# Layer crossings with their rows, gated outputs and scaled chunks in PSUM banks, part of the squares added by TensorE, and three slots first

## The chip, the cores and the metric

One core of a Trainium2 chip runs the whole program. The time is the device time of one execution in microseconds. The engines are TensorE (PE in the profile), VectorE (DVE), ScalarE (ACT), GpSimd (POOL) and SyncE (SP).

## The reference, cut to what matters

The program computes one hybrid block on 512 tokens and then four layers on 512 latent and 256 context tokens, 1024 features wide: windowed attention (layer 0), MLA (1), mLSTM (2), windowed attention (3). What the change touches is what stands between two of the four layers:

```python
for i in range(4):
    h_l = rmsnorm(x_lat, g_pre) * (1.0 + sc_l) + sh_l
    h_c = rmsnorm(x_ctx, g_pre) * (1.0 + sc_c) + sh_c
    y_l, y_c = mixer(h_l, h_c, ...)          # begins with h @ w_in, ends with (...) @ w_out
    x_lat = x_lat + gt_l * rmsnorm(y_l, g_post)
    if need_ctx:
        x_ctx = x_ctx + gt_c * rmsnorm(y_c, g_post)
```

A crossing, as it is called here, is from `@ w_out` of one layer to `@ w_in` of the next, in latent tokens (512 columns, LAT) and in context tokens (256 columns, CTX). There are three. In each, for each of the two parts: the squares of y are summed over 1024 features and give one rstd a token; y is gated and added to x; the squares of the new x are summed and give the next rstd; x is scaled, shifted and split into a high and a low part for the products.

## The kernel before

Activations lie feature-major: 8 chunks (KC) of 128 features, tokens along the columns. fp32 products are made of three fast products of high and low parts (`products`, L459 to L461). Weights come in slots of 1 MB in one fixed stream. Three ring places hold slots (a fourth slot of each output projection has its own place). For each slot SyncE issues the load once the slot before it in its place is used up, ScalarE makes the high part (`refill_hi`, L454; the tile after which it does so is in `refills`), and GpSimd the low part (`low_part`, L446), in the order of the stream.

`dense` (L486) runs one or more sections. TensorE makes the tiles in order, each in the next of `n_banks` PSUM banks, and waits for the bank's last user. ScalarE takes each tile out (`act_tile`); with `dve_tile` VectorE works on it next and frees the bank. If `n_banks` differs from the section before, TensorE first waits until all banks are free. With `lead` n the first n tiles are made together, chunk by chunk, each chunk when `rhs_ready` says that its low part is there. A `side` object puts work between the tiles: `half_tensor` in the middle of a tile, `on_tensor` after one, `on_scalar` after ScalarE's taking, `on_vector` ahead of VectorE's part, `after_scalar` and `after_vector` at the end. Everything on one engine runs in the order in which it is written.

`layer_cross` (L2744) runs the output projection on 7 banks: 8 latent tiles, then 8 context tiles. VectorE squares each latent tile and adds it to `total` (L2787, L2788); for the context ScalarE squares from PSUM (L2779) and VectorE adds (L2785). `LatentCrossing` stands as a side in the context tiles 8 to 15:

- TensorE sums `total` over the partitions with ones (`sum_up`, L2572) after tile 8, into bank 7. ScalarE makes rstd (`root`: Ln, L971, and Exp, L974), VectorE gates y in place and adds it to x (`residual`, L2587 and L2592), two chunks a tile.
- ScalarE squares the new x into `wide` (L2598), VectorE gathers the squares in `total` (L2604, L2607), TensorE sums them in the middle of tile 15, ScalarE makes the second rstd after tile 14.
- VectorE scales into `wide` (L2614), ScalarE shifts and makes the high part (L2619), VectorE the low part (L2624), chunk by chunk, with four buffers in `wide`.

`ContextCrossing` does the same for 256 columns inside the next section: the MLA's input section `Bin` (2 slots), the mLSTM's value section `Cv` (4 slots, 24 tiles with 256 columns), layer 3's query section `A3q` (4 slots, 8 latent tiles). Its places are given by `hosted`. In `Bin` and `Cv` two slots are used for the latent tiles first, then the same two for the context tiles. `LatentSteps` is the MLA's own side work; it stands in `Bz`.

## Time and profile before

| | |
|---|---|
| median of 3 runs | 2998.2 us (2993.7 to 3003.2) |
| the profiled execution, its span | 3006.05 us, 3004.4 us |
| TensorE busy | 2799.1 us, 93% |
| VectorE busy | 1571.7 us, 52% |
| ScalarE busy | 1231.1 us, 41% |
| GpSimd busy | 880.1 us, 29% |
| TensorE's mean granted clock | 0.976 of full |

Shares are of the span. A timeline row has the start in us, the time in us, engine, line, operation, output <- inputs, sizes and, in brackets, how long the engine stood before it and who ended that. "x2" is two instructions in a row, with one time for both. Weight loads of TensorE have rows of their own, named PEld. The three crossings begin at 1668, 2090 and 2598 us.

### The profile page before, as it was taken

How to read it: one execution, taken by the hardware profiler on the slowest of the kernel's cores; microseconds unless marked ns; L12 is line 12 of the kernel's file. 1: busy time of each engine (PE TensorE's matmuls, PEld its weight loads, DVE VectorE, ACT ScalarE, POOL GpSimd, SP SyncE). 2: the span in 40 equal slices, each digit the busy share in tenths (PEclk: the TensorE clock that was granted, in tenths of full speed). 3: DMA queues.
4: the chain of work that ended last, by engine and by line, in shares of the span. 5: the costliest groups of instructions: out<-in, count | busy, mean ns of one | idle time of the engine just before them, and what ended most of it. 6: DMA issues, size and time to landing. Idle time of an engine off the chain costs nothing.

```text
span 3004.4 us, 40540 instructions
## 1 busy us (share of the span) xinstructions
PE 2799.1 (93%) x16296; PEld 2329.7 (78%) x16296; DVE 1571.7 (52%) x3138; ACT 1231.1 (41%) x2139; POOL 880.1 (29%) x636
## 2 busy tenths in 40 slices
PE   6989989999999999999999979999899999989997
PEld 4766878778877788878877768677798998878785
DVE  6677290162942776660278461354627238562583
ACT  4335224453213222242278354544443326343582
POOL 3611564404543444423300123200223320124301
PEclk8999999999999999999999989999999999999998
DMA  7303452301323555531200221101112331123101
GB/s 312 138 28 120 182 210 84 112 1 70 128 101 129 215 190 191 204 147 71 92 15 2 78 81 67 43 1 57 71 58 71 142 126 55 71 85 127 49 2 70
DMA packets 55450, 300.09 MB, mean 100 GB/s; under 512 B 4640, under 2 KB 9056, under 8 KB 25440
## 3 DMA queue, kind: packets, MB, share of 16 engines
q1 hardware_dynamic: 22464, 163.59, 15.2%
q10 hardware_dynamic: 32800, 133.92, 11.8%
q8 instruction: 129, 2.11, 0.3%
q14 instruction: 57, 0.47, 0.0%
HBM read 271.25 MB, written 21.00 MB: 97 GB/s over the span
## 4 chain that ended last, share of the span: by engine, by line
PE 57%; DVE 11%; ACT 3%; issue 2%; DMA 0%; PEldq 0%; DVEq 0%; PEld 0%; ACTq 0%
PE psum L459 14%; PE psum L460 14%; PE psum L461 14%; PE psum L1889 2%; PE psum L3510 2%; PE psum L1729 2%; PE psum L1752 2%; PE psum L1910 2%; DVE pair_row L1943 1%; PE psum L1899 1%; DVE y L2587 1%; PE psum L1733 1%; PE psum L1741 1%; DVE total L2607 1%; DVE pair_prob L1952 1%
## 5 line engine op out<-in xcount | busy, mean ns | idle before, releaser
L446 POOL TENSOR_TENSOR w_lo<-raw,w_hi 128x512 fp32r<-128x512 f32 x612 | 853.6, 1426 | 2065.7 <-ACT w_hi L454 2065.7
L459 PE MATMUL psum<-a_hi,w_hi 128*128 128x512 f32 (+1 forms) x1848 | 697.6, 377 | 50.3 <-DVE a_lo L1132 18.4
L460 PE MATMUL psum<-a_lo,w_hi 128*128 128x512 f32 (+1 forms) x1848 | 686.6, 372 | 0.0
L461 PE MATMUL psum<-a_hi,w_lo 128*128 128x512 f32 (+1 forms) x1848 | 686.2, 371 | 0.0
L459 PEld LDWEIGHTS psum<-a_hi,w_hi 128*128 128x128 f32 x1848 | 350.7, 190 | 122.5 <-issue 24.1
L460 PEld LDWEIGHTS psum<-a_lo,w_hi 128*128 128x128 f32 x1848 | 350.8, 190 | 63.2 <-issue 3.4
L461 PEld LDWEIGHTS psum<-a_hi,w_lo 128*128 128x128 f32 x1848 | 350.4, 190 | 61.7
L454 ACT ACTIVATE w_hi<-raw 128x2048 fp32r<-128x2048 f32 x153 | 292.5, 1912 | 250.1 <-DMA raw<-stream 217.3
L459 PE MATMUL psum<-w_hi,a_hi 128*128 128x256 f32 x800 | 232.8, 291 | 4.9 <-DVE a_lo L2624 4.2
L460 PE MATMUL psum<-w_lo,a_hi 128*128 128x256 f32 x800 | 228.1, 285 | 0.0
L461 PE MATMUL psum<-w_hi,a_lo 128*128 128x256 f32 x800 | 228.0, 285 | 0.0
L875 DVE SCALAR_TENSOR_TENSOR ada_temp<-ada_ring,psum 128x1024 f32<-128x1024 f32 x160 | 185.7, 1215 | 29.3 <-ACT psum L1104 15.2
L459 PEld LDWEIGHTS psum<-w_hi,a_hi 128*128 128x128 f32 x800 | 155.1, 194 | 8.5 <-issue 5.1
L460 PEld LDWEIGHTS psum<-w_lo,a_hi 128*128 128x128 f32 x800 | 155.4, 194 | 1.6 <-issue 1.4
L461 PEld LDWEIGHTS psum<-w_hi,a_lo 128*128 128x128 f32 x800 | 155.3, 194 | 0.0
L875 DVE SCALAR_TENSOR_TENSOR ada_temp<-ada_ring,ada_rows 128x1024 f32<-128x1024 f32 x80 | 129.4, 1674 | 35.7 <-DVEq L1481 16.0
L1943 DVE CUSTOM_DVE_ANT_0 pair_row<-psum,pair_mask,neg_sinks 128x512 f32<-128x512 f32 (+2 forms) x160 | 116.6, 747 | 41.0 <-PE psum L1889 28.0
L1971 ACT ACTIVATE pair_prob<-pair_row,pair_stat 128x513 f32<-128x513 f32 (+2 forms) x160 | 114.8, 719 | 45.7 <-PE psum L1899 25.8
L1889 PE MATMUL psum<-gk,gq 64*128 64x128 f32 (+1 forms) x960 | 94.8, 330 | 13.3 <-DVE pair_stat L1943 11.5
L459 PE MATMUL psum<-hid_hi,w_hi 128*128 128x512 f32 x256 | 99.8, 390 | 0.0
L460 PE MATMUL psum<-hid_lo,w_hi 128*128 128x512 f32 x256 | 99.6, 389 | 0.0
L461 PE MATMUL psum<-hid_hi,w_lo 128*128 128x512 f32 x256 | 99.6, 389 | 0.0
(430 smaller groups left out, 4736.9 us busy)
## 6 DMA issues: line engine op xcount, KB each, us to landing
raw<-stream SPq DMA_DIRECT2D x153, 1024.0 KB, 4.8
ada_ring<-ada ACTq DMA_DIRECT2D x72, 1024.0 KB, 5.8
x_in<-xres ACTq DMA_DIRECT2D x3, 3072.0 KB, 12.5
xres<-x_in ACTq DMA_DIRECT2D x3, 2048.0 KB, 6.8
gates<-gate_part ACTq DMA_DIRECT2D x8, 768.0 KB, 3.9
partner<-gq ACTq DMA_DIRECT2D x4, 1024.0 KB, 9.2
xres<-x_in ACTq DMA_DIRECT2D x1, 3072.0 KB, 9.4
own_raw<-stream SPq DMA_DIRECT2D x3, 1024.0 KB, 5.0
```

The lines of the kernel that those rows point to most:

```text
L446: last = pool.tensor_tensor(k.lo_of(s)[:, cols], k.raw_of(s)[:, cols], k.hi_of(s)[:, cols].bitcast(F32), ALU.subtract)
L454: act.activation(k.hi_of(s), k.raw_of(s), ACT.Copy).then_inc(k.hi_ready, 1)
L459: pe.matmul(out, lhs[0], rhs[0], start=start, stop=False)
L460: pe.matmul(out, lhs[0], rhs[1], start=False, stop=False)
L461: return pe.matmul(out, lhs[1], rhs[0], start=False, stop=stop)
L875: dve.scalar_tensor_tensor(self.temp[:, self.products % 2], self.ring[:, place, c], 1.0, self.used_rows[:, w], ALU.mult, ALU.mult, accum_o ...
L1729: pe.matmul(score(u)[:, col:col + cols], q, keys, start=True, stop=False)
L1752: last = pe.matmul(value_bank(u), units[u]["pv"][j], prob_t[:, u % n_t, j * P:(j + 1) * P], start=j == 0, stop=j == n_blocks - 1)
L1889: last = pe.matmul(score(u)[:, col:col + cols], q, keys, start=True, stop=True)
L1910: last = pe.matmul(k.psum[64 * (u % 2):64 * (u % 2) + 64, 7, 0:P], units[u]["pv"][j], prob_t[:, u % 4, j * P:(j + 1) * P], start=j == 0, s ...
L1943: dve.tensor_tensor_reduce(row[:, u % 4, 1:1 + w], score(u), mask[:, un["mask"]:un["mask"] + w], 1.0, un["sink"], ALU.add, ALU.min, stat[: ...
L1971: act.activation(prob[:, u % 4, 0:1 + width(u)], row[:, u % 4, 0:1 + width(u)], ACT.Exp, bias=stat[:, 0, u % 4:u % 4 + 1], scale=-1.0, acc ...
```

## The change

In words, and then the diff cut to its core:

- Tiles keep banks 0 to 3 (`n_banks=4`) in the output projection and in the sections that follow it (`Bin` and `Bz`, `Cv`, the sections of layer 3). Bank 4 holds sums and then rstd of the latent part, bank 5 those of the context; banks 6 and 7 (`held`) hold gated outputs, two chunks in turn, and then scaled chunks.
- TensorE adds the last latent square to `total`, all 8 context squares of y straight from `square_c`, three of the 8 squares of the new latent x, and all 8 of the new context x. VectorE gathers five latent squares only (`GATHERED`).
- The latent sum stands in the middle of tile 8 and of tile 14; ScalarE's roots stand ahead of its taking of tiles 8 and 15 (`early_scalar`). VectorE's crossing work stands in one piece after its last latent square.
- The next section's third slot is made ready at the end of the crossing, and three slots are used for the latent tiles and then for the context tiles in `Bin` with the first of `Bz` (the two are one section now), and in `Cv`.

```diff
@@ dense
+                        if side is not None and 2 * (j + 1) == len(slot_tiles[0][1]):
+                            side.half_tensor(pe, 0)
...
+                    if side is not None:
+                        side.early_scalar(act, t)
                     if act_tile is not None:
                         act.wait_ge(done.sem, done_at(t))
-                        act_tile(act, i, tt, bank(t)).then_inc((free if dve_tile is None else staged).sem, 1)
+                        act_tile(act, i, tt, bank(t)) \
+                            .then_inc((free if dve_tile is None or t >= dve_until else staged).sem, 1)
...
-                if dve_tile is not None:
+                if dve_tile is not None and t < dve_until:
@@ class Crossing
+        self.sums = self.rstd = k.psum[:, 4 + n, 0:self.w]
...
+    def held(self, c):
+
+        return self.k.psum[:, 6 + c % 2, 0:self.w]
...
     def root(self, act, turn):
+
+        act.preload_act_table_set("natural_log")
         act.wait_ge(self.summed.sem, self.summed.at(turn + 1))
-        root_rows(self.k, act, self.rstd, [(self.t0, self.t1)], D, (7,))
-        act.nop().then_inc(self.rooted.sem, 1)
+        self.k.act_chain(act, act.activation(self.logs, self.sums, ACT.Ln, bias=self.k.eps[:], scale=1.0 / D))
+        act.activation(self.rstd, self.logs, ACT.Exp, scale=-0.5).then_inc(self.rooted.sem, 1)
...
         for j in (c, c + 1):
-            y = self.part(self.y, j)
-            gated = k.dve_chain.mark(dve.scalar_tensor_tensor(y, y, k.gate2[:, self.l, j, self.n:self.n + 1],
-                                                              self.rstd[:, self.t0:self.t1], ALU.mult, ALU.mult))
+            if j >= 2:
+                dve.wait_ge(self.added.sem, self.added.at(j - 1))
+            gated = k.dve_chain.mark(dve.scalar_tensor_tensor(self.held(j), self.part(self.y, j),
+                                                              k.gate2[:, self.l, j, self.n:self.n + 1], self.rstd,
+                                                              ALU.mult, ALU.mult))
...
+    def scale(self, dve, c):
+        if c == 0:
+            dve.wait_ge(self.rooted.sem, self.rooted.at(2))
+        if c >= 2:
+            dve.wait_ge(self.low.sem, self.low.at(c - 1))
+        dve.scalar_tensor_tensor(self.held(c), self.part(self.x, c), self.coef(c), self.rstd,
+                                 ALU.mult, ALU.mult).then_inc(self.scaled.sem, 1)
@@ class LatentCrossing
+    def half_tensor(self, pe, t):
+        k, q = self.k, t - KC
+        if q == 0:
+            pe.wait_ge(k.tile_free.sem, self.tile_free + KC)
+            pe.matmul(self.sums, k.cst("ones"), self.total, start=True, stop=False)
+            pe.matmul(self.sums, k.cst("ones"), self.last_square, start=False, stop=True).then_inc(self.summed.sem, 1)
+        if q >= 1:
+            self.context.sum_square(pe, q - 1)
+        if q == 6:
+            pe.wait_ge(self.gathered.sem, self.gathered.at(GATHERED))
+            pe.wait_ge(self.squared.sem, self.squared.at(KC - 1))
+            pe.matmul(self.sums, k.cst("ones"), self.total, start=True, stop=False)
+            for c in range(GATHERED + 1, KC):
+                if c == KC - 1:
+                    pe.wait_ge(self.squared.sem, self.squared.at(KC))
+                last = pe.matmul(self.sums, k.cst("ones"), self.wide[:, c % 4], start=False, stop=c == KC - 1)
+            last.then_inc(self.summed.sem, 1)
+
+    def early_scalar(self, act, t):
+        if t == KC:
+            self.root(act, 0)
+        if t == KC + 7:
+            self.root(act, 1)
...
     def after_vector(self, dve):
+        self.residual(dve, 0)
+        self.residual(dve, 2)
+        self.gather(dve, 1)
+        self.residual(dve, 4)
+        self.gather(dve, 2)
+        self.gather(dve, 3)
+        self.residual(dve, 6)
+        self.gather(dve, 4)
+        self.norm(dve)
@@ class ContextCrossing
+    def sum_square(self, pe, c):
+        k = self.k
+        pe.wait_ge(k.tile_free.sem, self.tile_free + KC + c + 1)
+        last = pe.matmul(self.sums, k.cst("ones"), self.own_squares[:, c % 4], start=c == 0, stop=c == KC - 1)
+        last.then_inc((self.partial if c < KC - 1 else self.summed).sem, 1)
+
+    def half_tensor(self, pe, t):
+        if t == 0:
+            self.sum_square(pe, KC - 1)
...
         if t == self.sum_at:
-            self.sum_up(pe, 0)
...
+            pe.wait_ge(self.squared.sem, self.squared.at(KC))
+            for c in range(KC):
+                last = pe.matmul(self.sums, k.cst("ones"), self.wide[:, c], start=c == 0, stop=c == KC - 1)
+            last.then_inc(self.summed.sem, 1)
+
+    def early_scalar(self, act, t):
+        if t == 0:
             self.root(act, 0)
-        if t == self.square_at:
             for c in range(KC):
-                self.square(act, c)
+                act.wait_ge(self.added.sem, self.added.at(c + 1))
+                act.activation(self.wide[:, c], self.part(self.x, c), ACT.Square).then_inc(self.squared.sem, 1)
             self.store_part(act)
-        if t == self.again_at - 1:
+        if t == self.root_at:
             self.root(act, 1)
-            for c in range(KC):
+        if t in self.high_at:
+            for c in range(*self.high_at[t]):
                 self.take_high(act, c)
@@ layer_cross
-          visits=[(s, feature_major(b, KC, [part])) for part in (LAT, CTX) for s in range(4)], own=3,
-          refills={0: [first + 2], 2: [first + 3], KC + 3: [first + 4], KC + 5: [first + 5]})
+    dense(k, block, [section], None, act_tile=take, dve_tile=add_square, side=latent, barrier=False, n_banks=4,
+          visits=[(s, feature_major(b, KC, [part])) for part in (LAT, CTX) for s in range(4)], own=3, dve_until=KC,
+          refills={0: [first + 2], 2: [first + 3], KC + 3: [first + 4], KC + 6: [first + 5]})
@@ gqa_layer (layer 3)
-        crossing[1].hosted(0, 1, 4)
+        crossing[1].hosted(3, 4, {5: (0, 4), 6: (4, 8)})
...
-          n_banks=BANKS if both else 7, side=crossing and crossing[1])
+          n_banks=BANKS if both else 4, side=crossing and crossing[1],
+          refills=None if both else {2 * s - 2: [SECTIONS[f"A{l}q"][0] + s + 1] for s in range(2, 5)})
@@ mla_layer
+    context.hosted(3, 4, {5: (0, 4), 6: (4, 8)})
...
+    dense(k, block, ["Bin", "Bz"], None, act_tile=take_in, barrier=False, lead=2, n_banks=4,
+          side=BothSides(context, steps, 11),
+          visits=[(s, feature_major(a, KC, [part])) for part in both for s in range(3)]
+          + [(s, feature_major(a, KC, both)) for s in range(3, 6)],
+          refills={9: [first + 3], 12: [first + 4], 14: [first + 5], 17: [first + 6], 21: [first + 7]})
@@ mlstm_layer
-    dense(k, block, ["Cv"], None, barrier=False, lead=2, n_banks=7, side=context, act_tile=take_value,
+    context.hosted(7, 9, {10: (0, 4), 11: (4, 8)})
...
+    dense(k, block, ["Cv"], None, barrier=False, lead=4, n_banks=4, side=context, act_tile=take_value,
+          visits=[(s, token_major(a, bs, 256, 256)) for bs in (range(4), (4, 5)) for s in range(3)]
+          + [(3, token_major(a, range(6), 256, 256))],
+          refills={15: [first + 3], 18: [first + 4], 20: [first + 5]})
```

## Rows read from the trace of the kernel before

**Rows 1.** Who waited for whom, TensorE, whole span: us, times, longest.

```profile
PE psum L2572 <- DVE total L2607: 39.0, 6, 8.7
```

**Rows 2.** Timeline of TensorE: first product of each of the three crossings.

```profile
1668.39 0.47 PE L459 MATMUL psum<-a_hi,w_hi 128*128 128x512 f32 x1 [0.47 <-PEq L386]
...
2089.89 0.47 PE L459 MATMUL psum<-b_hi,w_hi 128*128 128x512 f32 x1 [0.46 <-PEq L386]
...
2597.89 0.47 PE L459 MATMUL psum<-b_hi,w_hi 128*128 128x512 f32 x1 [0.74 <-DVEq L391]
```

**Rows 3.** Timeline of ScalarE: a tile taken out; last ones of the sections after.

```profile
1706.80 0.60 ACT L2772 ACTIVATE y<-psum 128x512 f32<-128x512 f32 x1 [4.84 <-PE psum L461]
...
1800.36 0.38 ACT L3034 ACTIVATE m_raw<-psum 128x256 f32<-128x256 f32 x1 [2.49 <-PE psum L461]
...
2252.07 0.39 ACT L3356 ACTIVATE cv<-psum 128x256 f32<-128x256 f32 x1 [2.50 <-PE psum L461]
...
2731.22 0.60 ACT L2828 ACTIVATE gq<-psum 128x512 f32<-128x512 f32 x1 [1.81 <-PE psum L461]
```

**Rows 4.** Timeline of TensorE in crossing 1: its long waits.

```profile
1743.35 2.08 PE L2572 MATMUL psum<-total,const 128*128 128x512 f32 x2 [8.71 <-DVE total L2607]
...
1750.79 0.47 PE L459 MATMUL psum<-a_hi,w_hi 128*128 128x512 f32 x1 [2.81 <-DVE a_lo L2624]
...
1780.53 1.22 PE L2572 MATMUL psum<-total,const 128*128 128x256 f32 x2 [8.34 <-DVE total L2607]
```

**Rows 5.** Stretch: us, busy PE, PEld, DVE, ACT, POOL, granted clock, DMA share, GB/s.

```profile
1735.00:1751.00 16.00, 4.85 (x15) 3.55 (x16) 12.74 (x13) 9.51 (x14) 9.13 (x6) 0.68 0.35 131
```

**Rows 6.** Timeline of TensorE: a ones-product, and the second product behind it.

```profile
1714.91 1.02 PE L2572 MATMUL psum<-total,const 128*128 128x512 f32 x2
...
1715.89 0.28 PE L460 MATMUL psum<-a_lo,w_hi 128*128 128x256 f32 x1
```

**Rows 7.** Timeline of VectorE: residual adds without and beside GpSimd.

```profile
1721.12 1.28 DVE L2592 TENSOR_TENSOR x_in<-x_in,y 128x512 f32<-128x512 f32 x2
...
1731.71 3.49 DVE L2592 TENSOR_TENSOR x_in<-x_in,y 128x512 f32<-128x512 f32 x2
```

**Rows 8.** By line: duration in ns min/median/max, first and last start in us.

```profile
L2334 DVE TENSOR_TENSOR psum<-psum,r x32: 690/698/700, 978.5 to 1274.6; 128x512 f32<-128x512 f32 x32
...
L2787 DVE TENSOR_TENSOR square<-y x24: 682/692/1393, 1680.9 to 2642.3; 128x512 f32<-128x512 f32 x24
...
L875 DVE SCALAR_TENSOR_TENSOR ada_temp<-ada_ring,psum x160: 1206/1215/1223, 16.1 to 1306.7; 128x1024 f32<-128x1024 f32 x160
```

**Rows 9.** Timeline of ScalarE: the first latent root of crossing 1.

```profile
1715.78 1.28 ACT L971 ACT_TABLE_LOAD   x1
1717.08 0.69 ACT L971 ACTIVATE rstd_y<-psum,eps 128x512 f32<-128x512 f32 x1
1717.78 1.28 ACT L974 ACT_TABLE_LOAD   x1
```

**Rows 10.** A slot's high part, low part and load (last number: us to landing).

```profile
L454 ACT ACTIVATE w_hi<-raw 128x2048 fp32r<-128x2048 f32 x153 | 292.5, 1912 | 250.1 <-DMA raw<-stream 217.3
...
1676.69 5.04 POOL L446 TENSOR_TENSOR w_lo<-raw,w_hi 128x512 fp32r<-128x512 f32 x4 [173.78 <-ACT w_hi L454]
...
raw<-stream SPq DMA_DIRECT2D x153, 1024.0 KB, 4.8
```

**Rows 11.** Timeline: VectorE begins to scale; one of ScalarE's high parts.

```profile
1748.17 0.75 DVE L2614 SCALAR_TENSOR_TENSOR wide<-x_in,coef,rstd_y 128x512 f32<-128x512 f32 x1 [2.94 <-ACTq L2578]
...
1751.34 0.72 ACT L2619 ACTIVATE a_hi<-wide,mod 128x512 fp32r<-128x512 f32 x1 [0.60 <-DVE wide L2614]
```

**Rows 12.** Timeline of VectorE: gated context outputs of two groups in a row.

```profile
1767.22 0.88 DVE L2587 SCALAR_TENSOR_TENSOR y<-y,gate,rstd_y 128x256 f32<-128x256 f32 x2 [7.75 <-ACTq L2578]
...
1768.69 0.88 DVE L2587 SCALAR_TENSOR_TENSOR y<-y,gate,rstd_y 128x256 f32<-128x256 f32 x2
```

**Rows 13.** Chain of waits: start us, us, what; between gate and residual add.

```profile
1721.27 0.45 issue
```

More of the change, by code:

```diff
@@ L509, in dense @@
     total = n_t * turns
+    dve_until = total if dve_until is None else dve_until
     share = ada.share(total) if ada else None
@@ L2591, in residual @@
             x = self.part(self.x, j)
[L2592 to L2607 removed]
+            dve.tensor_tensor(x, x, self.held(j), ALU.add).then_inc(self.added.sem, 1)
     def scale(self, dve, c):
@@ L2618, in take_high @@
         act.wait_ge(self.scaled.sem, self.scaled.at(c + 1))
-        act.activation(self.part(self.a[0], c), self.spare(c), ACT.Identity, bias=self.shift(c)) \
+        act.activation(self.part(self.a[0], c), self.held(c), ACT.Identity, bias=self.shift(c)) \
             .then_inc(self.high.sem, 1)
@@ L2623, in take_low, with norm @@
         dve.wait_ge(self.high.sem, self.high.at(c + 1))
-        dve.scalar_tensor_tensor(self.part(self.a[1], c), self.spare(c), self.shift(c),
+        dve.scalar_tensor_tensor(self.part(self.a[1], c), self.held(c), self.shift(c),
                                  self.part(self.a[0], c).bitcast(F32), ALU.add, ALU.subtract) \
             .then_inc(self.low.sem, 1)
+    def norm(self, dve):
+        self.scale(dve, 0)
+        for c in range(KC):
+            if c + 1 < KC:
+                self.scale(dve, c + 1)
+            self.take_low(dve, c)
     def store_part(self, act):
@@ L2646, in at, with over, square @@
         return self.base + n
+GATHERED = 4
 class LatentCrossing(Crossing):
-    def on_tensor(self, pe, t):
-        if t == KC:
-            self.sum_up(pe, 0)
-    def half_tensor(self, pe, t):
-        if t == 2 * KC - 1:
-            self.sum_up(pe, 1)
+    def over(self, context, total, last_square, own_squares, tile_free, late):
+        self.context, self.total, self.last_square, self.own_squares = context, total, last_square, own_squares
+        self.tile_free, self.late = tile_free, late
+    def half_tensor(self, pe, t):
[16 more added lines that the diff above has]
+    def early_scalar(self, act, t):
+        if t == KC:
+            self.root(act, 0)
+        if t == KC + 7:
+            self.root(act, 1)
+    def square(self, act, c):
+        act.wait_ge(self.added.sem, self.added.at(c + 1))
+        if c >= 4:
+            act.wait_ge(self.gathered.sem, self.gathered.at(max(1, c - 4)))
+        act.activation(self.wide[:, c % 4], self.part(self.x, c), ACT.Square).then_inc(self.squared.sem, 1)
     def on_scalar(self, act, t):
         q = t - KC
-        if q == 0:
-            self.root(act, 0)
         if 1 <= q <= 4:
@@ L2695, with gather @@
-class ContextCrossing(Crossing):
-    def hosted(self, sum_at, square_at, again_at):
-        self.sum_at, self.square_at, self.again_at = sum_at, square_at, again_at
+        refill_hi(self.k, act, self.late)
+    def gather(self, dve, c):
+        dve.wait_ge(self.squared.sem, self.squared.at(c + 1))
+        if c == 1:
+            dve.tensor_tensor(self.total, self.wide[:, 0], self.wide[:, 1], ALU.add).then_inc(self.gathered.sem, 1)
+            return
+        dve.wait_ge(self.gathered.sem, self.gathered.at(c - 1))
+        dve.tensor_tensor(self.total, self.total, self.wide[:, c % 4], ALU.add).then_inc(self.gathered.sem, 1)
@@ L2726, in on_vector @@
     def on_vector(self, dve, t):
-        if t:
-            return
-        for c in range(0, KC, 2):
-            self.residual(dve, c)
-            if c:
-                self.gather(dve, max(1, c - 2))
-                if c > 2:
-                    self.gather(dve, c - 1)
-        self.gather(dve, KC - 2)
-        self.gather(dve, KC - 1)
-        for c in range(KC + 1):
-            if c < KC:
-                self.scale(dve, c)
-            if c:
-                self.take_low(dve, c - 1)
+        if t == 0:
+            dve.wait_ge(self.latent.low.sem, self.latent.low.at(KC))
+            for c in range(0, KC, 2):
+                self.residual(dve, c)
+            self.norm(dve)
 def layer_cross(k, block, l, section, b, a, y_at, x_at, temp):
     y, x = k.at("y", y_at, [P, KC, T2]), k.at("x_in", x_at, [P, KC, T2])
-    total = k.at("total", temp, [P, T2])
-    rstd = k.at("rstd_y", temp + 3072, [P, T2])
+    total = k.at("total", temp, [P, S])
+    logs = k.at("rstd_y", temp + 3072, [P, T2])
     square = k.at("square", temp + 6144, [P, 2, S])
@@ L2768, in layer_cross @@
     start = k.tile_free.base
+    first = SECTIONS[section][0]
+    latent = LatentCrossing(k, l, 0, y, x, a, logs[:, 0:S], wide)
+    context = ContextCrossing(k, l, 1, y, x, a, logs[:, S:T2], wide_c)
+    context.over(square_c, start, latent)
+    latent.over(context, total[:], square[:, (KC - 1) % 2], square_c, start, first + 6)
     def take(act, i, t, ps):
@@ L2974, in over, with __init__, half_tensor, on_tensor @@
             x.stage_over(n)
+class BothSides(Side):
+    def __init__(self, context, steps, at):
+        self.context, self.steps, self.at = context, steps, at
+    def half_tensor(self, pe, t):
+        self.context.half_tensor(pe, t)
+    def on_tensor(self, pe, t):
+        self.context.on_tensor(pe, t)
+        if t >= self.at:
+            self.steps.on_tensor(pe, t - self.at)
+    def early_scalar(self, act, t):
+        self.context.early_scalar(act, t)
+        if t == self.at:
+            self.context.after_scalar(act)
+    def on_scalar(self, act, t):
+        if t >= self.at:
+            self.steps.on_scalar(act, t - self.at)
+    def on_vector(self, dve, t):
+        self.context.on_vector(dve, t)
+        if t >= self.at:
+            self.steps.on_vector(dve, t - self.at)
 class QueryTurns(Side):
```

117 lines of the change are left out of this document (37 added, 80 removed).

## The prediction

> **What bounds the kernel now.** I read the list of who waited for whom on TensorE first. Over the whole span one wait stands on top of those the change can touch: the two-stage sum that closes each layer crossing waits for VectorE's adds, 39.0 us in 6 waits [rows 1]. There are three crossings. From the timeline I took where each begins (first product of the output projection) and where the section that receives the context half ends [rows 2, 3]. A 512-column tile takes 4.84 + 0.60 = 5.44 us from one eviction to the next, a 256-column tile 2.89 us [rows 3]; both are TensorE's pace. Against that pace:
>
> - Crossing 1, projection and the first MLA section: 12 tiles of each size = 99.9 us; it took 1800.8 - 1668.4 = 132.4. Excess 32.5 us.
> - Crossing 2, projection and the value section of 24 small tiles: 43.5 + 92.5 = 136.0; it took 2252.1 - 2089.9 = 162.2. Excess 26.2.
> - Crossing 3, projection and the query section of 8 large tiles: 110.2; it took 2731.2 - 2597.9 = 133.3. Excess 23.1.
>
> So 82 us in all are above TensorE's own pace. In crossing 1 TensorE waited 8.7 us for the latent sum, 2.8 for the first low part and 8.3 for the context sum [rows 4], and between 1735 and 1751 us its granted clock was 0.68 of full, so part of the stretch at 1.2 GHz and not 2.4, after the 8.7 us wait [rows 5]. That is the room. Why the sum is late shows on VectorE: two residual adds took 1.28 us while GpSimd was idle and 3.49 while it worked [rows 7].
>
> **What the change adds to TensorE.** A ones-product of 512 columns holds TensorE from 1714.91 to 1715.89, less the 0.12 of the product between (2.89 / 24): 0.86 us; 256 columns half, 0.43 [rows 6]. Per crossing before: two of each, 2.6 us. After: latent rows 2, context rows 8 small, latent new rows 4 (total and three squares), context new rows 8 small: 6 x 0.86 + 16 x 0.43 = 12.0 us, say 12.4 with the breaks. The added 9.8 us are in TensorE's stream and only pay where it stood idle anyway.
>
> **What it does to the latent chain.** An operand in PSUM costs VectorE nothing at this size: 698 ns in PSUM against 692 between SBUF tiles, and 160 operations with a PSUM operand spread from 1206 to 1223 ns only, so GpSimd doesn't disturb them [rows 8]. The context squares leave VectorE. I go through crossing 1 in its own times.
>
> 1. TensorE stops in the middle of context tile 0 (1713.5) for the last square, adds 1.75 us and gives the sum at 1715.5. ScalarE roots before it takes that tile: Ln 0.69, table load 1.28 [rows 9], Exp by estimate like Ln, 0.65: VectorE starts at 1718.3, 1.5 us earlier than now. Tile 1's break waits for the late taking, with the first wait 0.9 us.
> 2. VectorE: four pairs of residual at 2.65 us (four operations of 0.66), four adds of squares of 0.7: done at 1732 to 1733; ScalarE's last square at 1733.4.
> 3. TensorE reaches the middle of tile 6 at 1735.7 with 1.75 + 6 x 0.43 us of ones inside. Nothing waits. Four ones-products: 1739.7; the tile ends at 1741.2.
> 4. ScalarE may root only when it has taken tile 6 and made a high part: 0.66 + 1.91 [rows 10], then load, Ln, load, Exp, 3.9 us: 1747.7. Now VectorE starts scaling at 1748.17 [rows 11]. All that was won on VectorE is handed over at this place. The first low part comes at 1750.2 instead of 1750.8.
> 5. TensorE ends tile 7 at 1744.3 and stands 5.9 us. So per crossing: one wait of 5.9 for 8.7 + 2.8, and 9.8 more work.
> 6. The next section's first tiles follow the low parts. ScalarE's high parts come every 0.72 + 0.60 = 1.32 us [rows 11]; a bank that must be read before it is written again adds about 0.1. TensorE needs 1.36 per chunk, so little is lost, but after 5.9 us idle I expect the low clock for some 3.4 us of it: 1.7 us. Bounds: 0 and 3.
>
> By the end of the first tiles crossing 1 is where it was before (within 0.5 us).
>
> **Context half, crossings 1 and 3.** Root from 1761.7 to 1765.2 (after the high parts and a slot's high part of 1.91; two loads 2.56 and by estimate 0.9 for Ln and Exp at half the width of rows 9), then four groups of VectorE, 1.47 us each now [rows 12] and 1.6 with the bank waits: squares end at 1772.3. TensorE has tiles 2 and 3 until 1774.1. The wait of 8.3 us is gone. In crossing 1 the high parts 4 to 7 are made only after tile 5 is taken; the context tile that reads them loses 1.7 us (bounds 0, 3). Then the slot that follows three resident ones: free after tile 7, landed 4.8 us later, high part after tile 9 (5.8 + 0.4), 1.91, low part 5.04 [rows 10], 13.3 us against four tiles of 2.89 = 11.5: TensorE stands 1.8 us (bounds 0, 4). Another 0.8 for the clock.
> Crossing 1: 12.4 + 0.9 + 5.9 + 2.0 + 1.7 + 1.8 + 0.8 = 25.5 against 32.5: **-7.0**.
> Crossing 3 has neither of the last three (its context tiles come a section later): 12.4 + 0.9 + 5.9 + 1.9 = 21.1 against 23.1: **-2.0**.
>
> **Crossing 2.** Here the first four tiles run together and there are four banks. ScalarE makes the context root and all eight squares before it takes tile 0; TensorE needs tile 0's bank for tile 4. Behind that wait stands everything on TensorE, the context sum too. First tiles end at 2185.3 (four times 2.89, one break, the clock). ScalarE: high parts end 2180.8, slot 1.91, two loads 2.56, Ln and Exp at half the width of rows 9 by estimate 0.9: 2186.3; VectorE 6.4; last square and taking 2193.6. A new wait of 8.3 us, and 2.0 for the clock after it. Bounds: 6 (no bank waits) and 12. High parts 0.5, late slot 1.8, waiting for all banks when the next section changes from 4 to 7 banks 0.7.
> 12.4 + 0.9 + 5.9 + 1.7 + 8.3 + 2.0 + 0.5 + 1.8 + 0.7 = 34.2 against 26.2: **+8.0**.
>
> **Sum.** -7.0 - 2.0 + 8.0 = -1.0 us. Against the profiled execution's 3006.1 (span 3004.4) that is 3005.1. The runs' median is 2998.2, 7.9 under the profiled one, so I predict 2997.
>
> **Two rules of the Trainium skill.** The first: the trace shows two table loads of 1.28 us in a root, one ahead of Ln and one ahead of Exp [rows 9]. The Trainium skill, ScalarE: Activation LUTs, section "Table sets: the hidden batching unit", says that one set holds both ln and exp, so that one load serves both. The change asks for a set ahead of Ln; were it one with both, a load would go at each root (a rival below). The second: VectorE: DVE Perf Modes, section "The TRN2 errata", again the Trainium skill, charges a VectorE operation from PSUM 120 cycles instead of 58 from SBUF, by estimate 0.065 us more; on some 17 operations of the latent chain that would be 1 us more per crossing. The rows say 698 against 692 ns, and by them nothing is added.
>
> **Rivals.**
> - *Clock and waits at their kind ends (faster).* After a shorter idle of 5.9 us the clock doesn't fall, and the bank waits cost nothing: 3 x 1.8 + 2.0 + 0.8 of clock and about 2 of crossing 2's wait: -10.2, in all -11: 2987. For it: each idle is shorter than 8.7 us. Against it: the clock is low in rows 5 over a wait of 2.8 us too.
> - *Two banks make a ping-pong (slower).* From gate to add the chain shows 0.45 us in which the engine waited for nothing seen [rows 13]. If each handing over of a bank costs that and not 0.05, the latent norm is 8 x 0.4 = 3.2 us longer and TensorE follows it: 9.6 over three crossings, and 3 in crossing 2's new wait: +12.6, in all +11.6: 3010. It decides from some 0.3 us per chunk on. Against it: VectorE's own rows run without a gap across its chained waits.
> - *It doesn't do what it says.* GpSimd slows the operations with PSUM operands as it does the others: about 1 us in the residual beyond the 2.2 us to spare at step 3, and 2 in the norm beside the second slot's low part: +3 per crossing, 3006. Rows 8 speak against it.
> - *One table load per root.* The one ahead of Exp goes: 1.28 us on the second latent root of three crossings and on the context root of crossing 2: -5.1, in all -6: 2992. The rule is the Trainium skill's, named above; the trace has two loads each time.
>
> **How the numbers follow.** Forecast 0.50, kind ends 0.22, ping-pong 0.15, GpSimd 0.06, one load 0.07. A change of under 0.3% (9 us) can't be told from none here. Faster: the 0.22 and 0.05 from the forecast's own spread: 0.27. Slower: 0.15, 0.03 of the GpSimd case, 0.03 of the forecast's: 0.20 with rounding. The same: 0.53. Low and high end reach to the two outer cases: 2985 to 3011; the forecast's own range is 2990 to 3004.
>
> **What would show it.** Right: the waits of the latent and context sums for VectorE gone; one wait of 5 to 7 us ahead of each following section, released by a low part; TensorE idle 6 to 12 us at the value section's fifth tile with ScalarE's taking as releaser; 1 to 3 us for a low part from GpSimd at the fourth slot of the MLA and value sections; residual adds of 1.3 us per pair also beside GpSimd. Wrong: the second latent root before 1745 in crossing 1's times (then about 3 us per crossing more are won), no wait at the fifth tile (8 to 10 us more), or a high part every 1.7 us or more.

## The result, and the profile after

The changed kernel takes 3006.38 us (median of 16 runs, 3003.6 to 3010.0) against 2999.80 us of the kernel before (16 runs, 2992.7 to 3003.9): a ratio of 1.0023, 95% interval 1.0016 to 1.0030. It is slower by 6.6 us. The forecast was 2997 us, no measurable change. A later repetition of the unchanged pair on another chip (below) gives 1.0026.

The profiled execution of the kernel after has a span of 3003.1 us and an own time of 3005.17. TensorE is busy 2818.9 us (before 2799.1), VectorE 1520.2 (1571.7), ScalarE 1227.9, GpSimd 870.7; the mean granted clock is 0.981 (0.976).

The waits of TensorE in the kernel after, whole span (us, times, longest):

```profile
PE psum L459 <- DVE a_lo L2616: 17.4, 6, 5.6
...
PE psum L459 <- POOL w_lo L446: 13.5, 6, 4.8
...
PE psum L3590 <- DVE c_decay L3697: 10.4, 9, 1.6
...
PE psum L459 <- ACT cv L3436: 6.9, 2, 6.4
...
PE psum L2984 <- ACTq L2974: 2.6, 1, 2.6
```

The 39.0 us for sums [rows 1] are gone. The places of the others, in the timeline of TensorE; these rows answer to [rows 4]:

```profile
1747.25 0.77 PE L459 MATMUL psum<-a_hi,w_hi 128*128 128x512 f32 x1 [5.56 <-DVE a_lo L2616]
...
1807.58 0.50 PE L459 MATMUL psum<-a_hi,w_hi 128*128 128x512 f32 x1 [1.61 <-POOL w_lo L446]
...
1829.78 1.53 PE L2984 MATMUL psum<-squares,const 128*128 128x512 f32 x4 [2.63 <-ACTq L2974]
...
2164.49 0.55 PE L459 MATMUL psum<-w_hi,a_hi 128*128 128x256 f32 x1 [5.55 <-DVE a_lo L2616]
...
2185.35 0.56 PE L459 MATMUL psum<-w_hi,a_hi 128*128 128x256 f32 x1 [6.41 <-ACT cv L3436]
...
2680.43 0.77 PE L459 MATMUL psum<-a_hi,w_hi 128*128 128x512 f32 x1 [5.56 <-DVE a_lo L2616]
```

Each crossing ends in one wait of 5.6 us, released by a low part, and the value section has the new wait at its fifth tile. What stands ahead of the first of them is the timeline of ScalarE and, last, VectorE in crossing 1:

```profile
1738.43 0.38 ACT L2814 ACTIVATE y<-psum 128x256 f32<-128x256 f32 x1 [6.07 <-PE psum L461]
1738.71 0.38 ACT L2821 ACTIVATE square_c<-psum 128x256 f32<-128x256 f32 x1
1738.98 1.91 ACT L454 ACTIVATE w_hi<-raw 128x2048 fp32r<-128x2048 f32 x1
1740.91 1.28 ACT L2580 ACT_TABLE_LOAD   x1
1742.21 0.69 ACT L2582 ACTIVATE rstd_y<-psum,eps 128x512 f32<-128x512 f32 x1
1742.91 1.28 ACT L2583 ACT_TABLE_LOAD   x1
...
1744.84 1.41 DVE L2606 SCALAR_TENSOR_TENSOR psum<-x_in,coef,psum 128x512 f32<-128x512 f32 x2 [16.36 <-ACT psum L2583]
```

VectorE stood 16.36 us; its gathering had ended at 1728.5. All of its lead is lost at ScalarE, whose order is: take tile 6, convert a slot, root.

GpSimd, in turn, begins its low parts only when VectorE's latent adds are over, 0.19 us after the last of them. It is so in all three crossings of both profiles of after. The end of VectorE's gathering and GpSimd's start in crossing 1:

```profile
1727.80 0.69 DVE L2709 TENSOR_TENSOR total<-total,wide 128x512 f32<-128x512 f32 x1
...
1728.68 5.02 POOL L446 TENSOR_TENSOR w_lo<-raw,w_hi 128x512 fp32r<-128x512 f32 x4 [38.21 <-ACT w_hi L454]
```

Cut at the same events as [rows 2] and [rows 3] (first product of each projection; last tile of mz, cv, gq taken out), every profile taken in this study falls into seven stretches. "Crossing" is a projection with the section behind it. All in us:

| | start to 1 | crossing 1 | 1 to 2 | crossing 2 | 2 to 3 | crossing 3 | tail | three crossings |
|---|---|---|---|---|---|---|---|---|
| before | 1668.4 | 204.5 | 217.0 | 162.2 | 345.8 | 133.3 | 273.2 | 500.0 |
| before_again | 1667.6 | 201.4 | 219.0 | 158.9 | 345.9 | 132.0 | 272.9 | 492.2 |
| before_third | 1666.1 | 205.3 | 216.9 | 162.1 | 345.8 | 130.2 | 273.3 | 497.6 |
| before_fourth | 1665.4 | 205.3 | 216.9 | 162.1 | 345.8 | 130.3 | 273.3 | 497.6 |
| after | 1665.9 | 199.6 | 217.6 | 168.2 | 347.7 | 131.3 | 272.7 | 499.2 |
| after_again | 1663.5 | 199.6 | 221.2 | 168.2 | 347.8 | 131.3 | 272.7 | 499.0 |

The profile that the prediction was made from has the dearest crossings of four profiles of the same kernel; the changed kernel's repeat to 0.1 us. Their mean before is 496.9, after 499.1.

### The profile page after: what moved, and what is told of

Its sections match the earlier page's. It is cut to its first block, busy times and chain, and to the rows that moved or that the text cites. A ratio compares the mean times of both kernels' runs of the same rounds, so it can differ in the third digit from the quotient of the medians.

```text
span 3003.1 us, 40627 instructions
## 1 busy us (share of the span) xinstructions
PE 2818.9 (94%) x16404; PEld 2344.5 (78%) x16404; DVE 1520.2 (51%) x3081; ACT 1227.9 (41%) x2139; POOL 870.7 (29%) x636
## 4 chain that ended last, share of the span: by engine, by line
PE 59%; DVE 8%; ACT 3%; issue 1%; DMA 1%; POOL 0%; PEldq 0%; DVEq 0%; PEld 0%; ACTq 0%
PE psum L459 15%; PE psum L460 15%; PE psum L461 15%; PE psum L1898 2%; PE psum L1738 2%; PE psum L3590 2%; PE psum L1761 2%; PE psum L1919 2%; DVE pair_row L1952 1%; PE psum L1908 1%; PE psum L1742 1%; PE psum L1750 1%; DVE pair_prob L1961 1%; ACT w_hi L454 0%; DVE c_decay L3697 0%
## 5 line engine op out<-in xcount | busy, mean ns | idle before, releaser
L446 POOL TENSOR_TENSOR w_lo<-raw,w_hi 128x512 fp32r<-128x512 f32 x612 | 844.1, 1411 | 2074.0 <-ACT w_hi L454 2074.0
```

The costliest lines, as they stand in the source:

```text
L446: last = pool.tensor_tensor(k.lo_of(s)[:, cols], k.raw_of(s)[:, cols], k.hi_of(s)[:, cols].bitcast(F32), ALU.subtract)
```

## The experiments

The repetitions of before and before_splits_late start from the kernel before, every other experiment from the kernel after. Ratios are to runs of before on the same chip, with 95% intervals.

**before_again and after_again: the unchanged pair.**

> The kernel before, unchanged, for a second trace. Theory A (the profiled execution of before was a slow one of its kind): the three crossings take again 132.4, 162.2 and 133.3 us within 1 us each, and the span lies 4 to 8 us under 3004.4, the difference being spread over stages the change doesn't touch. Theory B (the crossings of before usually cost less than in that one trace): the same difference lies inside the three crossings, mainly as stretches at full clock that were at the low one. Time ratio 1.000.

> The changed kernel, unchanged. Both theories: ratio to before 1.002. A: crossings with their following sections take 199.6 (to the end of the MLA input), 168.2 and 131.3 us again within 1 us, the rest of the span varies by some us. B: the crossings vary, the rest doesn't.

Measured: 2999.94 us, ratio 1.0007 (0.9997 to 1.0016), and 3004.80 us, ratio 1.0026 (1.0017 to 1.0036). The loss is real. Theory B holds for the kernel before: its crossings cost 7.8 us less in this profile than in the first, mostly in waits, while the rest of its span is 0.9 us longer. For the kernel after it fails: the crossings repeat to 0.1 us, and the stretch between crossings 1 and 2 moves, by 3.6 us. The waits for the latent sum, timeline of TensorE in before_again, against 8.71 three times in before ([rows 4] has the first):

```profile
1739.32 1.22 PE L2572 MATMUL psum<-total,const 128*128 128x512 f32 x1 [5.47 <-DVE total L2607]
...
2159.60 2.08 PE L2572 MATMUL psum<-total,const 128*128 128x512 f32 x2 [5.47 <-DVE total L2607]
...
2667.56 2.07 PE L2572 MATMUL psum<-total,const 128*128 128x512 f32 x2 [8.71 <-DVE total L2607]
```

And what stands ahead of the shorter wait. GpSimd in before at the place of [rows 7], then GpSimd and VectorE in before_again at the same place:

```profile
1731.29 6.71 POOL L446 TENSOR_TENSOR w_lo<-raw,w_hi 128x512 fp32r<-128x512 f32 x4 [38.30 <-ACT w_hi L454]
```

```profile
1730.51 13.93 POOL L446 TENSOR_TENSOR w_lo<-raw,w_hi 128x512 fp32r<-128x512 f32 x8 [38.30 <-ACT w_hi L454]
...
1730.93 1.29 DVE L2592 TENSOR_TENSOR x_in<-x_in,y 128x512 f32<-128x512 f32 x2
1732.13 2.39 DVE L2607 TENSOR_TENSOR total<-total,wide 128x512 f32<-128x512 f32 x2
```

GpSimd starts 0.42 us ahead of the adds in both profiles, but the same two adds take 1.29 us here and 3.49 there. What decides between the two isn't shown.

**before_third and before_fourth: how often.**

> The kernel before, unchanged, for one more profile. Theory, the crossings of before vary with who holds the SBUF operands first, VectorE or GpSimd: of the three waits for the latent sum some are 5.5 and some 8.7 us, nothing between, and the three crossings add up to 490 to 500 us, while the rest of the span stays within 3 us of the other two. Rival, the spread sits elsewhere (the clock's stretches behind the first crossing): all three waits 8.7 and crossings of 500 us.

> As before_third: the same kernel once more, for the share of the two lengths of the wait.

Measured, one run each: 3001.32 and 3000.60 us. Both have 8.7, 8.7 and 5.5; of the twelve waits in four profiles eight are 8.7 and four 5.5, with nothing between, as the theory said. The wait alone doesn't fix the stretch (crossing 3 takes 133.3 and 132.0 us with 8.71): the granted clock behind it differs too.

**before_splits_late: GpSimd moved away from the gathering.**

```diff
# the kernel before, layer_cross
-          refills={0: [first + 2], 2: [first + 3], KC + 3: [first + 4], KC + 5: [first + 5]})
+          refills={0: [first + 2], 2: [first + 3], KC + 4: [first + 4], KC + 6: [first + 5]})
```

> The kernel before, with the last two weight slots of a crossing's section (own part of the next section) converted one tile later, so that GpSimd's low parts start 5.4 us later and run beside the scaling and not beside the gathering of the squares. Theory A, the wait of TensorE for the latent sum (8.7 us in all three crossings of one profile of before; 5.5, 5.5 and 8.7 in the other) is VectorE slowed by GpSimd on SBUF operands: the wait falls to 1 to 3 us in every crossing and no longer varies; the first low chunk behind it may wait 1 to 4 us longer, so the time is 2986 to 2998 us. Rival, GpSimd has no part in it and the spread has another cause: the wait stays at 5.5 to 8.7, and with the late slots the time is 3000 to 3010 us.

Measured: 2996.36 us, ratio 0.9984 (0.9975 to 0.9993). The timeline of TensorE, crossing 1; the other two have the same 1.55 and 8.90:

```profile
1732.50 1.12 PE L2572 MATMUL psum<-total,const 128*128 128x512 f32 x2 [1.55 <-DVE total L2607]
...
1743.95 0.77 PE L459 MATMUL psum<-a_hi,w_hi 128*128 128x512 f32 x1 [8.90 <-DVE a_lo L2624]
```

The sum's wait is 1.55 us in all three crossings: it was VectorE beside GpSimd. The edit also moves ScalarE's conversions, but in before VectorE works from 1719.8 to 1745.2 us without a gap, so no late square held it up. What was dear there were its own operations beside GpSimd, and in this run none of the latent adds stands beside GpSimd. But the contention goes to the scaling, where VectorE now takes up to 1.75 us an operation and not 0.74:

```profile
1740.38 1.75 DVE L2614 SCALAR_TENSOR_TENSOR wide<-x_in,coef,rstd_y 128x512 f32<-128x512 f32 x1
...
1746.06 0.74 DVE L2614 SCALAR_TENSOR_TENSOR wide<-x_in,coef,rstd_y 128x512 f32<-128x512 f32 x1
```

So 11.5 us of waiting (8.71 + 2.81) became 10.45: a small gain, from two numbers in the old kernel. The wait for the first low chunk grew by 6.1 us, where 1 to 4 had been expected.

**cv_take_first: the value section's fifth tile.**

```diff
     def early_scalar(self, act, t):
         if t == 0:
             self.root(act, 0)
+        if t == self.square_at:      # 4 in the value section, 0 elsewhere
             for c in range(KC):
...
```

> The changed kernel, but in the value section of the mLSTM ScalarE makes the eight context squares ahead of taking tile 4 and not of tile 0. Theory (the new wait of 6.4 us at the fifth tile is the price of crossing 2): the wait falls to under 1 us, and with it the clock that is low after it: crossing 2 takes 160 to 162 us and not 168, the kernel is 6 to 8 us faster than the changed one, about level with before. Rival (TensorE's added ones-products and not the wait make crossing 2 slower; the wait is given back later, at the late slot): no more than 2 us faster.

Measured: 2996.76 us, ratio 0.9992 (0.9983 to 1.0001), 8.0 us under after_again on the same chip; crossing 2 falls from 168.2 to 159.6. The wait of 6.41 us at 2185.35 is 0.6. That this wait is the price of crossing 2, and that it costs 8.6 us with the clock behind it, is shown.

**root_early and refill_early: the second root.**

```diff
-        if t == KC + 7:              # root_early only
+        if t == KC + 6:
             self.root(act, 1)
...
-          refills={0: [first + 2], 2: [first + 3], KC + 3: [first + 4], KC + 6: [first + 5]})
+          refills={0: [first + 2], 2: [first + 3], KC + 3: [first + 4], KC + 5: [first + 5]})
```

> The changed kernel, but ScalarE makes the second latent root ahead of taking tile 14 and not of tile 15, and the next section's second slot gets its high part after tile 13 and not after 14. Theory (what is won on VectorE is handed over on ScalarE, which roots only after taking tile 14 and a high part): VectorE starts to scale 5 us earlier, TensorE's wait ahead of each following section falls from 5.6 us to about 2, with less low clock behind it: 4 to 5 us per crossing, 12 to 15 us faster than the changed kernel. Rival (the norm's own pace of VectorE and ScalarE, 1.45 us a chunk, sets the time of the next section): under 5 us in all.

> The kernel after with the conversion of the last weight slot (1.91 us on ScalarE) one tile earlier, and the second root where it was. It splits the gain of root_early (-7.8 us, C1 -3.9, C2 -3.1, C3 -3.3). Theory: the chain from tile 14 to the first low chunk is serial on ScalarE, so 1.9 us of the 5.6 go in each crossing: 5.7 us less than the kernel after, a ratio to before of 1.0005; the rest of root_early's gain is the root's earlier place. Rival: the root waits for the latent sum as well, which stands in the middle of tile 14, and the conversion hides behind that: 0 to 2 us less, a ratio of 1.002.

Measured: root_early 2997.05 us, ratio 0.9997 (0.9988 to 1.0005), 7.8 us under after_again, where 12 to 15 had been expected (crossings 195.7, 165.1 and 128.0, together 10.3 us less); refill_early (the second edit alone) 3001.22, ratio 0.9994 (0.9985 to 1.0003), a little better than the expected 1.0005. In refill_early the wait of 5.56 us is 3.76 in all three crossings, 1.8 less, about as long as the conversion (1.91); the crossings take 5.5 us less. The root's place gives the other 4.8 us, the wait is then 2.2 (timeline of TensorE, combined, which has the same edit):

```profile
1744.64 0.47 PE L459 MATMUL psum<-a_hi,w_hi 128*128 128x512 f32 x1 [2.21 <-DVE a_lo L2616]
```

A wait of about 2 us is what had been expected; what the 12 to 15 us had too high is the price, 3.4 us a crossing for 3.4 us of wait and not 4 to 5. In crossing 2 part of the gain comes back as a wait at the fifth tile, which grows from 6.4 to 7.2 us. The 2.2 us stand there because ScalarE takes the projection's last tile before the first high part, as highs_early shows.

**steps_slots: three smaller waits.**

```diff
-        if t == self.at:
+        if t == self.at - 1:
             self.context.after_scalar(act)
...
-          side=BothSides(context, steps, 11),
+          side=BothSides(context, steps, 12),
...
-          refills={9: [first + 3], 12: ...
+          refills={8: [first + 3], 12: ...
...
-          refills={15: [first + 3], ...
+          refills={14: [first + 3], ...
```

> The kernel after with two edits only: the norm steps of MLA's low rank sections start one tile later, and the late slots of Bin and Cv are converted one tile earlier. Theory A: the 2.63 us wait of TensorE for the root of the steps goes to nothing, and the two waits for a low part of 1.6 us shrink to 0.1 to 0.5: 2.6 + 1.2 + 1.2 = 5 us less than the kernel after, 3000 us. Rival: the second step's root comes later too, the next section's first tile waits for the normed rows in its place, and the load of the late slot lands only 1 us before the old conversion: less than 1.5 us in all, 3004 us or more.

Measured: 3001.50 us, ratio 1.0000 (0.9991 to 1.0009). Crossing 1 takes 196.1 (-3.5) and crossing 2 166.2 (-2.0); the 2.63 us wait is gone, and those for w_lo fall from 13.5 to 10.9. 5.6 us less in these two crossings, where 5 had been expected; the wait at the fifth tile grows from 6.4 to 7.2 us here too.

**sums_twice: the price of TensorE's ones-products.** The context squares are added twice, so the context's root is another one.

```diff
     def sum_square(self, pe, c):
...
+        pe.matmul(self.sums, k.cst("ones"), self.own_squares[:, c % 4], start=c == 0, stop=False)
-        last = pe.matmul(self.sums, k.cst("ones"), self.own_squares[:, c % 4], start=c == 0, stop=c == KC - 1)
+        last = pe.matmul(self.sums, k.cst("ones"), self.own_squares[:, c % 4], start=False, stop=c == KC - 1)
```

> The kernel after with each of the eight products of ones that add the context's squares issued twice into the same bank (the sum of those squares comes out double, so the context's root is another). Eight products of 256 columns in full precision more per crossing, 24 in all, at 0.43 us (2.89 us of a 256-column tile over 24 products of a third of that each is 0.12 for one pass; these take four passes at 0.107). Theory A, TensorE's own pace is the bound wherever it does not wait, also in the crossings: 24 x 0.43 = 10.3 us more, 3015 us, and the wait for the first low chunk keeps its 5.6 us because the chain ahead of it starts with tile 14. Rival, the crossings are bound by the chain of roots and squares: the products fill the wait of 5.6 us, 0 to 3 us more, 3005 to 3008 us.

Measured: 3014.16 us (3012.5 to 3014.5), ratio 1.0043 (1.0029 to 1.0057). The crossings grow by 3.0, 2.7 and 2.4 us, 8.1 together for 24 products, 0.34 each; the price of 0.43 less what two waits give back (a_lo L2616: 17.4 us became 16.1, the fifth tile 6.4 became 5.9). By these stretches, which repeat to 0.1 us in after, the products are on the path for the most part, and the rival, that they fill the waits, falls. The runs alone would not settle it: the ratio is 0.0017 to 0.0020 over that of after, 5 to 6 us where 10.3 had been expected, with an interval of 4 us to each side.

**combined and highs_early: all of it, and one step more.** combined is cv_take_first, root_early and steps_slots together. highs_early adds:

```diff
         if t == KC + 6:
             self.root(act, 1)
+        if t == KC + 7:
+            self.take_high(act, 0)
+            self.take_high(act, 1)
...
     def after_scalar(self, act):
-        for c in range(KC):
+        for c in range(2, KC):
             self.take_high(act, c)
```

> The kernel after with four edits: Cv's context squares start behind the taking of tile 3 instead of ahead of tile 0 (alone: C2 168.2 to 159.6 us); the second latent root one tile earlier, with the refill before it (alone: C1 199.6 to 195.7, C2 168.2 to 165.1, C3 131.3 to 128.0); MLA's norm steps one tile later (the profile of the kernel after has a wait of 2.63 us of TensorE at 1829.78 us for them); the late slots of Bin and Cv converted one tile earlier (waits of 1.6 us each for GpSimd's low part). Theory A, the waits stand one behind the other on TensorE's path, so the gains add: C1 199.6 - 3.9 - 1.5 = 194.2, C2 168.2 - 8.6 - 3.1 - 1.5 = 155.0, C3 131.3 - 3.3 = 128.0, the stretch behind C1 less by 2.6, or the whole of it 21 us under the kernel after: 2984 to 2988 us. Theory B, one wait takes the place of the other (the first low chunk is then bound by the second root's own chain, and Cv's fifth tile moves with it): 2990 to 2995 us.

> The kernel combined, with the first two chunks' high parts taken ahead of the last tile of the projection. In combined TensorE waits 2.2 us in each of three crossings for the first low chunk, and ScalarE has stood 2.2 us before that for tile 15, with the scaled chunk ready. Theory: ScalarE's order is the whole of this wait, so it goes, in all three crossings: 6.6 us less than combined, 2975 to 2978 us where before is 3002, a ratio to before near 0.9915. Rival: the wait is the chain of the second root itself (sum, two table loads, Ln, Exp, scale, high, low), which ends at the same time, or the fill of the first tiles at one chunk per 1.45 us takes its place: 0 to 2 us less, a ratio of 0.993.

Measured: combined 2982.68 us (2975.3 to 2985.2), ratio 0.9936 (0.9924 to 0.9949), a little under the expected 2984 to 2988, its crossings 192.0, 155.7 and 128.1; highs_early 2973.50 us (2972.4 to 2977.1), ratio 0.9902 (0.9888 to 0.9915), its crossings 188.1, 153.3 and 124.1, 10.3 us less than combined where 6.6 had been expected. The gains add: alone they take 8.6, 10.3 and 5.3 us from the crossings, 24.2 in sum, together 23.3. The last step gives 3.9 us in crossing 1 and 4.0 in crossing 3 for a wait of 2.2 us in each; the other 1.7 us are clock, since in crossing 1 the same instructions are busy for 187.8 and then for 186.1 us. In crossing 2, where combined already has a granted clock of 1.00, it gives 2.4 us, what the waits lose (2.2 to 0.8 us, and 2.2 to 1.1 at the fifth tile). Crossings 1 and 2 as stretches (columns as in [rows 5]), in after:

```profile
1665.90:1865.50 199.60, 188.63 (x1018) 161.13 (x1018) 61.99 (x95) 85.14 (x123) 51.51 (x39) 0.98 0.22 80
2083.14:2251.36 168.22, 154.00 (x1004) 141.22 (x1004) 49.77 (x106) 63.34 (x104) 40.62 (x32) 0.96 0.23 82
```

in combined:

```profile
1665.94:1857.95 192.01, 187.81 (x1018) 160.24 (x1018) 58.66 (x95) 84.99 (x124) 49.89 (x39) 0.99 0.23 83
```

and in highs_early:

```profile
1669.53:1857.62 188.09, 186.09 (x1018) 158.88 (x1018) 58.65 (x95) 85.08 (x123) 49.81 (x39) 1.00 0.23 84
2077.33:2230.61 153.28, 149.85 (x1004) 136.86 (x1004) 49.82 (x106) 63.03 (x104) 40.68 (x32) 1.00 0.25 90
```

With no wait over 1.1 us left in the crossings the granted clock stays at 1.00, the level of 2.4 GHz. TensorE's 1018 instructions of crossing 1 need 186.1 us busy there, 188.6 in after. These two beat both kernels, highs_early by 1.0%.

## Why the prediction was wrong

The sum for the crossings came out right against the execution it was made from, in part by luck, and it was not the whole of the change. Step by step:

- *Steps 1 to 5, the latent chain.* In before's times (2.49 us later than after's) VectorE starts its residuals at 1718.2, forecast 1718.3, and its scaling at 1747.3, forecast 1747.7; TensorE waits 5.56, forecast 5.9. Right; only the gathering ends earlier, at 1731.0 and not 1732 to 1733. The claim that the lead on VectorE is handed over at ScalarE is what root_early and refill_early show.
- *An operand in PSUM costs nothing and isn't slowed by GpSimd.* Right, but not by the sign that was named. The pairs of latent residual adds take 1.28 us throughout, yet none stands beside GpSimd: the latent sum's wait went because VectorE is done 0.19 us before GpSimd begins. What shows the claim are operations that do stand beside it. Two gated outputs of 256 columns, before and after (the two kernels' VectorE rows, with GpSimd at work over all of each):

```profile
1771.59 2.90 DVE L2587 SCALAR_TENSOR_TENSOR y<-y,gate,rstd_y 128x256 f32<-128x256 f32 x2
```

```profile
1757.72 5.04 POOL L446 TENSOR_TENSOR w_lo<-raw,w_hi 128x512 fp32r<-128x512 f32 x4 [11.80 <-ACT w_hi L454]
...
1761.26 0.88 DVE L2593 SCALAR_TENSOR_TENSOR psum<-y,gate,psum 128x256 f32<-128x256 f32 x2 [4.64 <-ACT psum L2583]
```

  Alone such a pair takes 0.88 us in before too [rows 12]. The two scalings of 1744.84 stand beside GpSimd for most of their time as well and take 0.70 us each; of all 48 operations at line 2606 the longest takes 0.757 us, where scalings on SBUF took 1.75. Of the Trainium skill's 120 cycles from PSUM for 58 (VectorE: DVE Perf Modes, "The TRN2 errata"), which by estimate would be 0.065 us, the trace shows at most 0.02 (0.76 us against 0.74).
- *Ones-products.* Right in kind; sums_twice prices them at 0.34 us each net of the waits, near 0.43 before them.
- *Context half and late slots.* No wait for the context sum, as forecast. High parts 4 to 7 cost 0.6 us and not 1.7; the late slot 1.6 and not 1.8. **A term was missing**: MLA's norm steps start at tile 11 of a merged list, where a small tile stands between the root and its use, and TensorE waits 2.63 us. steps_slots takes it away.
- *Crossing 2.* Fifth tile 6.4 us and not 8.3, with the mechanism named; with its clock it is worth 8.6 (cv_take_first).
- *The clock.* Its terms, crossing by crossing, were 2.0 + 0.8, 1.7 + 2.0 and 1.9 us (with a little for the chunks' pace). The same instructions are busy 2.5, 4.2 and 2.1 us longer in after than in highs_early at a granted clock of 1.00. The price of 1.7 us for one low stretch came from no row; the steps of 1.7 us between crossings 1 and 2 (below) bear it out.
- *The sum.* -7.0, +8.0, -2.0 = -1.0 was forecast, against 204.5, 162.2 and 133.3. Measured: -4.9, +6.0, -2.0 = -0.9. That the sums agree is luck: crossing 1 wins 2.1 us less and crossing 2 loses 2.0 less than forecast.

**The step that failed is the last one, from the sum to the time: "-7.0 - 2.0 + 8.0 = -1.0 us", then "the runs' median is 2998.2, 7.9 under the profiled one, so I predict 2997".** It made two assumptions without a reason for either. The first is that the change costs nothing outside the crossings; there the changed kernels lose 4.2 us (next paragraph), the larger part of what was missed. The second is that what makes the profiled execution slow stays in the changed kernel. But 3.2 of the 7.9 us stood in the crossings (500.0 against the mean of 496.9 over four profiles), in waits of VectorE beside GpSimd that come in two lengths, and the change removes these. Against a usual execution the crossings cost 2.2 us more, not 1.0 less: crossing 1 gives 4.5, crossing 2 costs 6.9, crossing 3 gives 0.1.

**Two stretches outside the crossings were left out.** Between crossings 2 and 3 all nine profiles of changed kernels have 346.6 to 348.0 us, mean 347.6, the five of before and before_splits_late 345.8 to 345.9: +1.7. Of these, 0.47 is the wait when the value section's four banks give way to seven (forecast 0.7, but counted in crossing 2), and 1.0 more waiting for c_decay (10.4 us in 9 waits against 9.4 in 8); the rest is not found. Between crossings 1 and 2 the nine changed profiles have 217.6, five times 219.3 to 219.7 and three times 221.0 to 221.2, mean 219.8; the five others four times 216.9 to 217.0 and once 219.0, mean 217.4: +2.5. About 0.5 is the bank wait again; the steps of 1.7 are clock. The stretch in before and in after_again:

```profile
1872.93:2089.89 216.96, 208.84 (x1250) 157.66 (x1249) 95.43 (x231) 107.22 (x225) 16.26 (x12) 1.00 0.06 20
```

```profile
1863.10:2084.34 221.24, 212.44 (x1250) 159.56 (x1251) 95.95 (x232) 107.56 (x225) 17.77 (x14) 0.98 0.06 20
```

The same 1250 instructions are busy 3.6 us longer at 0.98. The low stretches stand at two places: behind a wait of TensorE of 1.7 to 2.0 us for mk (six of the nine, none of the five) and behind one of 2.06 us for pair_stat (five of the nine, one of the five). The kernel before has both waits too. In after_again the granted clock is 0.66 between 1896.5 and 1900.0 us, right behind the first. Why the changed kernels mostly get one or two where before mostly gets none stays open. The change edits no line of that work, but the stretch begins with the bank wait and has 14 of GpSimd's low parts in it and not 12; whether that matters wasn't tested. Together, as means over these profiles: crossings +2.2, 1 to 2 +2.5, 2 to 3 +1.7, start +0.4, tail -0.6, and 2.1 us around the span for 1.65, +0.4: 6.6, as measured. That it meets the 6.6 so closely is luck: single terms are known to about 1 us only, and the stretch ahead of crossing 1 alone varies from 1663.5 to 1670.0 us. The two profiles of after by themselves give +2.2, +2.0 and +1.9 for the first three terms, and spans only 3.5 us over before's.

The rivals: *kind ends* gave the clock as its reason, and that the clock recovers with short waits is true of highs_early, but with after's waits of 5.6 us the clock was low. *Ping-pong* had the time nearest to the result (3010) for a reason that isn't there: a chunk takes 1.445 us, forecast 1.42. *One table load* falls: the root keeps two, 1.28 us each.

## What to carry to other kernels

When the profiled execution lies above the median, find where its excess sits before the difference is carried over: if it sits in what the change removes, the change has already lost it; a second profile of the same kernel shows that at once. Give the stretches outside the changed ones a term too, if only a range: here they were put at nothing and lost 4.2 us. A chain that gets faster on one engine is worth nothing until the order written for the next engine is moved with it: here mainly a few positions in ScalarE's list turned a loss of 0.2% into a gain of 1.0%. When a wait of TensorE goes down to about 1 us, count the clock behind it as well, here 1.7 us beside a wait of 2.2 in two crossings and nothing in the third.

## What was not expected of the hardware

- VectorE beside GpSimd, both on SBUF, doesn't slow by a steady factor: with the same instructions and the same start to 0.01 us, counted from the crossing's start, the same two adds took 1.29 or 3.49 us, and the wait behind them 5.5 or 8.7 us, four and eight times in twelve. With an operand in PSUM a pair of gated outputs took 0.88 us beside GpSimd as alone, on SBUF 2.90. The latent adds say nothing on this, since in after they are over before GpSimd begins.
- Taking away a wait of 2.2 us gave 3.9 and 4.0 us in crossings 1 and 3, the clock included; in crossing 2, where the clock was at 1.00 already, two waits shorter by 2.5 us in sum gave 2.4. With waits up to 1.1 us the granted clock was 1.00 through all three crossings (highs_early). In crossing 1 it was 0.99 with one of 2.2 us (combined), 0.98 with waits of 5.6, 1.6 and 2.6 us (after) and 0.94 with 8.7, 2.8 and 8.3 us (before). A wait of 2.2 us does not always bring the clock down: crossing 2 of combined has two of them at 1.00.
